# First projections of two mixer layers as three products of high and low parts, with some low parts made by GpSimd

## What is computed

```
h   = norm-modulated rows: x * (1 + scale) + shift, from "ada" rows     768 x 1024
all = h @ w_in[l]                                                      1024 x 3840
      columns: q, f, b  three 256-wide inputs of a gated scan (a)
               ai       256, the scan's values
               b, c, d  three 512-wide sets of heads (queries, keys, values); cv 256, c's values
               g0, g1   1024, the output gate
y_a = decayed scan in both directions over q, f, b, ai
y_b, y_c, y_d = three kinds of attention, over tokens and context
x   = layer_norm(alpha * x + gate * ((concat(y_a..y_d) * silu(g)) @ w_out[l]))
```

## Time and profile before

| | us |
|---|---|
| three runs, median | 2365.77 |
| lowest, highest | 2362.79, 2371.43 |
| profiled execution, its own time | 2367.96 |
| its span, first to last instruction | 2365.9 |
| TensorE busy (matmuls) | 2090.8 (88%) |
| VectorE, ScalarE, GpSimd busy | 1153.6, 727.3, 56.7 |
| mean granted clock of TensorE | 0.94 of 2.4 GHz |

### The profile page before, as it was taken

The page is one execution under the profiler, slowest core; times in us unless marked ns, Lnnn a source line. Parts: engine busy times, 40 slices in busy tenths (PEclk is TensorE's granted clock), DMA queues, the critical chain, the costliest instruction groups (busy, mean ns, idle before and its releaser), DMA issues.

```text
span 2365.9 us, 24945 instructions
## 1 busy us (share of the span) xinstructions
PE 2090.8 (88%) x9184; PEld 1341.3 (57%) x9184; DVE 1153.6 (49%) x2688; ACT 727.3 (31%) x1612; POOL 56.7 (2%) x98
## 2 busy tenths in 40 slices
PE   5888998999789698898997859968899997999999
PEld 2644655544344364565554424535478885887887
DVE  1284273545445548164655365773644444333333
ACT  2212224544330122234543111113542323223222
POOL 2000000000000000000000200000000000000000
PEclk9899999999789899999998979987899998999999
DMA  8111011000451211111000512112033331333331
GB/s 259 35 34 48 23 36 36 10 27 27 152 214 54 50 54 36 36 45 36 26 11 10 161 47 63 48 42 54 1 89 98 91 106 54 90 97 98 98 97 64
DMA packets 149144, 157.18 MB, mean 66 GB/s; under 512 B 5725, under 2 KB 110337, under 8 KB 149025
## 3 DMA queue, kind: packets, MB, share of 16 engines
q1 hardware_dynamic: 142592, 135.81, 18.8%
q0 software_dynamic: 6432, 19.78, 3.0%
HBM read 151.37 MB, written 4.19 MB: 66 GB/s over the span
## 4 chain that ended last, share of the span: by engine, by line
PE 73%; DVE 16%; ACT 5%; issue 3%; DMA 2%; POOL 1%; DVEq 0%; ACTq 0%; SPq 0%; POOLq 0%
PE psum L704 15%; PE psum L1115 9%; PE psum L1116 9%; PE psum L1117 9%; PE psum L879 5%; PE psum L716 5%; PE psum L731 4%; PE psum L1013 4%; PE psum L917 3%; PE psum L893 3%; PE psum L667 2%; DVE stats L1860 2%; ACT arena L1380 1%; PE psum L749 1%; ACT arena L1212 1%
## 5 line engine op out<-in xcount | busy, mean ns | idle before, releaser
L704 PE MATMUL psum<-arena 128*128 128x512 f32 (+2 forms) x1536 | 557.4, 521 | 8.6 <-ACT arena L1212 4.6
L1212 ACT ACTIVATE arena<-psum 128x256 f32<-128x256 f32 (+6 forms) x524 | 205.8, 421 | 789.5 <-PE psum L667 236.7
L704 PEld LDWEIGHTS psum<-arena 128*128 128x128 f32 x1536 | 294.9, 200 | 234.2 <-issue 205.8
L1115 PE MATMUL psum<-part,part 128*128 128x512 f32 x896 | 351.6, 392 | 10.8 <-DVE part L2191 8.8
L1116 PE MATMUL psum<-part,part 128*128 128x512 f32 x896 | 351.2, 392 | 0.0
L1117 PE MATMUL psum<-part,part 128*128 128x512 f32 x896 | 350.9, 392 | 0.0
L2187 DVE TENSOR_TENSOR part<-arena,part 128x1024 fp32r<-128x1024 f32 x112 | 137.3, 1226 | 251.5 <-ACT part L1212 251.5
L1860 DVE TENSOR_REDUCE stats<-psum 128x1 f32<-128x768 f32 (+6 forms) x208 | 138.8, 709 | 164.6 <-PE psum L879 163.2
L1212 ACT ACTIVATE part<-arena 128x1024 fp32r<-128x1024 f32 (+1 forms) x176 | 151.4, 895 | 202.1 <-PE psum L1117 140.9
L1115 PEld LDWEIGHTS psum<-part,part 128*128 128x128 f32 x896 | 169.6, 189 | 47.4 <-issue 12.2
L1117 PEld LDWEIGHTS psum<-part,part 128*128 128x128 f32 x896 | 169.5, 189 | 35.4
(11 more groups left out here) (253 smaller groups left out, 1929.9 us busy)
## 6 DMA issues: line engine op xcount, KB each, us to landing
arena<-in_w_in SPq DMA_DIRECT2D x72, 512.0 KB, 4.3
arena<-in_w_mlp SPq DMA_DIRECT2D x64, 512.0 KB, 3.9
arena<-in_w_ada SPq DMA_DIRECT2D x48, 512.0 KB, 6.1
arena<-in_w_gate SPq DMA_DIRECT2D x32, 512.0 KB, 4.1
arena<-in_w_out SPq DMA_DIRECT2D x24, 512.0 KB, 3.7
arena<-in_w_in SPq DMA_DIRECT2D x20, 256.0 KB, 3.1
arena<-in_w_branch SPq DMA_DIRECT2D x8, 512.0 KB, 4.2
arena<-in_x POOLq DMA_DIRECT2D x4, 512.0 KB, 9.1
```

The source lines that it names most:

```text
L704: mm = pe.matmul(bank(b)[:, c0:c1], lhs[:, k, m * P:(m + 1) * P], ring.view(tag, l, k // 2)[:, k % 2, c0:c1], start=k == 0, stop=k == kt - 1)
L1115: pe.matmul(dst, lo, x_hi_, start=first, stop=False)
L1212: return act.activation(dst, src, ACT.Copy)
```

## The change

The q, f, b, ai, b, c, cv and d products of both layers (not the gate products, not `w_out`) become three products of fp32r parts each.

- **h**: modulation writes rows into `gated`; ScalarE copies them to `h_hi` (in h_t's place) and VectorE subtracts in place, giving `h_lo` (`split_rows`). At the attention stage VectorE adds the two again (`whole_rows`) for the gate products, tile by tile.
- **weights**: per layer 22 blocks (13 and 9; ai and cv now in 2 blocks of 4 k instead of 4 of 2). ScalarE makes every high part, in space that is free at the time (`HI_PLACES`). The low part goes into the ring slot: 6 + 5 by VectorE (the next stage's first block, and `SPLIT_WITH` more beside the hg products), 7 + 4 by GpSimd (`SPLIT_BEFORE`: before which tile of the stream).
- **order**: two tiles of the stream come ahead of the scan, then 18 fillers on 14 steps (t = 0) and 11 on 9 (t = 1) in place of 20 and 13 on 14. In t = 1 ScalarE may write key rows only after the last d product.
- the arena becomes three tensors at the same addresses.

```diff
-    def rows(key, w, c0, n):
+    def rows(key, w, c0, n, per=2):
         v = w.rearrange("(k p) n -> p k n", p=P)
-        for i in range(KT // 2):
-            ring.add(key + (i,), v[:, 2 * i:2 * i + 2, c0:c0 + n], (2, n))
+        for i in range(KT // per):
+            ring.add(key + (i,), v[:, per * i:per * i + per, c0:c0 + n], (per, n))
...
+                rows(("ai", l), w, C_AI, 256, 4)
...
+        HI_PLACES = (("free", "o", "v0", "v1", "q0", "q1", "free", "o", "v0", "v1", "q0", "q1", "v0"),
+                     ("free", "q0", "q1", "s0", "s1", "s2", "free", "s0", "s1"))
+        SPLIT_BEFORE = ({1: (6,), 2: (7,), 3: (8,), 6: (9, 10), 12: (11, 12)}, {1: (5,), 2: (6,), 6: (7, 8)})
+        SPLIT_WITH = (5, 4)
+        def block_before(l, t, j):
+            place = HI_PLACES[t][j]
+            earlier = [input_blocks(l, t)[i] for i in range(j) if HI_PLACES[t][i] == place]
+            if t == 1 and j == 0:
+                earlier = [input_blocks(l, 0)[i] for i in range(13) if HI_PLACES[0][i] == place]
+            return earlier[-1] if earlier else None
+        def parts_made(key):
+            t = 1 if key[0] in ("cv", "d") or key[0] == "hg" and key[2] == 1 else 0
+            beside = any(input_blocks(key[1], t).index(key) in js for js in SPLIT_BEFORE[t].values())
+            return (lo_pool if beside else lo_dve).at(key)
+        def input_parts(key):
+            n = ring.number(*key)
+            t = 1 if key[0] in ("cv", "d") or key[0] == "hg" and key[2] == 1 else 0
+            hi = hi_slots[HI_PLACES[t][input_blocks(key[1], t).index(key)]]
+            return [ap.rearrange("p (k n) -> p k n", k=ring.dims[n][0]) for ap in (hi, ring_lo[n % N_SLOTS])]
...
+            def product_of_parts(tag, l, m, b, last, c0, c1, first):
+                per = SLOT // WIDTH[tag]
+                for k in range(KT):
+                    key = (tag, l, k // per)
+                    hi, lo = input_parts(key)
+                    if first and k % per == 0:
+                        pe.wait_ge(*parts_made(key))
+                    x_hi_, w_hi, w_lo = h_hi[:, k, m * P:(m + 1) * P], hi[:, k % per, c0:c1], lo[:, k % per, c0:c1]
+                    pe.matmul(bank(b)[:, c0:c1], h_lo[:, m, k, :], w_hi, start=k == 0, stop=False)
+                    pe.matmul(bank(b)[:, c0:c1], x_hi_, w_lo, start=False, stop=False)
+                    mm = pe.matmul(bank(b)[:, c0:c1], x_hi_, w_hi, start=False, stop=k == KT - 1)
+                    if last and k % per == per - 1:
+                        mm.then_inc(mm_done(("weights", ring.number(*key))), 1)
...
-                        pe.wait_ge(*ring.landed("hg", l, t, name))
+                        pe.wait_ge(*lo_dve.at(("hg", l, t, name)))
                     last = (name, s) not in [(x[0], x[1] - 1) for x in hg_tiles(l)]
                     open_bank(s)
+                    hi, lo = input_parts(("hg", l, t, name))
                     for k in range(KT):
-                        mm = pe.matmul(bank(s)[:, 0:t1 - t0], ring.view("hg", l, t, name)[:, k, :], h_t[:, k, t0:t1], start=k == 0, stop=k == KT - 1)
+                        mm = product_3(bank(s)[:, 0:t1 - t0], hi[:, k, :], lo[:, k, :], h_hi[:, k, t0:t1], h_lo[:, t0 // P:t1 // P, k, :], k == 0, k == KT - 1)
...
+                        if tag == "g0":
+                            pe.wait_ge(*whole_dve.at("h", l, m))
...
+            def split_rows(l, m):
                 if l > 0:
                     act.wait_ge(*product_ready("out1", l - 1, m, last_q_of(l - 1) - 1))
-                v, b = 0 if m < LT else 1, 4 + (2 * m) % 4
-                for j in range(4):
-                    x = act.activation(h_t[:, j, m * P:(m + 1) * P], bank(b)[:, j * P:(j + 1) * P], ACT.Identity,
-                                       bias=ada_t[:, l, j, v:v + 1], scale=ada_t[:, l, 8 + j, v:v + 1])
-                x.then_inc(h_act(("h", l, m)), 1)
+                act.wait_ge(*h_act.at("h", l, m))
+                act.wait_ge(*h_dve.at("h", l, m))
+                copy(h_hi[:, :, m * P:(m + 1) * P], h_rows[:, m]).then_inc(xhi_act(("h", l, m)), 1)
+            def split_input(l, t, j):
+                key = input_blocks(l, t)[j]
+                act.wait_ge(*ring.landed(*key))
+                if block_before(l, t, j) is not None:
+                    act.wait_ge(*mm_done.at("weights", ring.number(*block_before(l, t, j))))
+                copy(input_parts(key)[0], ring.view(*key)).then_inc(hi_act((key,)), 1)
...
+                    if n < SPLIT_WITH[t]:
+                        split_input(l, t, n + 1)
...
+                        if t == 1:
+                            act.wait_ge(*mm_done.at("weights", ring.number("d", l, KT // 2 - 1)))
...
+                    for j in SPLIT_BEFORE[t].get(p, ()):
+                        split_input(l, t, j)
...
-                    alongside(scan(l, t), 14, beside, 20 if t == 0 else 13)
+                    next(beside)
+                    alongside(scan(l, t), 14 if t == 0 else 9, beside, 18 if t == 0 else 11)
+                    if t == 0:
+                        split_input(l, 1, 0)
...
+            def split_rows(l, m):
+                dve.wait_ge(*xhi_act.at("h", l, m))
+                dve.tensor_tensor(h_lo[:, m], h_rows[:, m], h_hi[:, :, m * P:(m + 1) * P].bitcast(F32), ALU.subtract).then_inc(xlo_dve(("h", l, m)), 1)
+            def whole_rows(l, m):
+                cols = slice(m * P, (m + 1) * P)
+                dve.tensor_tensor(h_t[:, :, cols], h_hi[:, :, cols].bitcast(F32), h_lo[:, m].bitcast(F32), ALU.add).then_inc(whole_dve(("h", l, m)), 1)
+            def split_input(l, t, j):
+                key = input_blocks(l, t)[j]
+                hi, lo = input_parts(key)
+                dve.wait_ge(*hi_act.at(key))
+                dve.tensor_tensor(lo, ring.view(*key), hi.bitcast(F32), ALU.subtract).then_inc(lo_dve((key,)), 1)
...
-                for _ in range(8 * last_q_of(l)):
+                whole_rows(l, 0)
+                for i in range(8 * last_q_of(l)):
+                    if i % 4 == 0 and i // 4 + 1 < last_q_of(l):
+                        whole_rows(l, i // 4 + 1)
...
+                            if l < DEPTH - 1 and m >= 2:
+                                split_rows(l + 1, m - 2)
...
+                    split_rows(l + 1, last_q - 2)
                     modulate(l + 1, last_q - 1)
+                    split_rows(l + 1, last_q - 1)
+                    split_input(l + 1, 0, 0)
...
             for m in range(TT):
+                if m >= 1:
+                    split_rows(0, m - 1)
                 modulate(0, m)
+            split_rows(0, TT - 1)
+            split_input(0, 0, 0)
...
-                    for tag, m in stream_tiles(t):
+                    for p, (tag, m) in enumerate(stream_tiles(t)):
+                        for j in SPLIT_BEFORE[t].get(p, ()):
+                            key = input_blocks(l, t)[j]
+                            hi, lo = input_parts(key)
+                            pool.wait_ge(*hi_act.at(key))
+                            pool.tensor_tensor(lo, ring.view(*key), hi.bitcast(F32), ALU.subtract).then_inc(lo_pool((key,)), 1)
                         if tag in HEADS and LT <= m < last_q_of(l):
                             nq = HEADS[tag][0] * HEADS[tag][2]
                             q_dst = {"b": q_b, "c": q_c, "d": q_d}[tag][:, m, :]
```

More of the change, by code:

```diff
@@ L238, in build, with __init__ @@
         class Region:
-            def __init__(self, start, size):
-                self.start, self.size, self.at = start, size, 0
+            def __init__(self, start, size, tensor, first):
+                self.start, self.size, self.at, self.tensor, self.first = start, size, 0, tensor, first
             def reset(self):
@@ L247, in cut @@
                 assert self.at + n <= self.size, (self.at, n, self.size)
-                ap = base[:, self.start + self.at:self.start + self.at + n]
+                ap = self.tensor[:, self.first + self.at:self.first + self.at + n]
                 self.at += n
@@ L315, in build @@
         att = R_WORK.cut(2, TT, P)
-        key_rows, states = R_WORK.cut(TT + LT + 2 * CT, P), R_WORK.cut(TT + 4, P)
+        states = R_WORK.cut(TT + 4, P)
+        key_rows_at = R_WORK.start + R_WORK.at
+        key_rows = R_WORK.cut(TT + LT + 2 * CT, P)
         e_q, e_k = R_WORK.cut(2, SEQ), R_WORK.cut(2, CTX)
-        R_WORK.cut(2 * TT * SEQ + 2 * CT * CTX - (4 * TT + LT + 2 * CT + 4) * P - 2 * TOK)
-        q_s, kf_s, kb_s, o_a = R_WORK.cut(TOK), R_WORK.cut(TOK), R_WORK.cut(TOK), R_WORK.cut(TT, 256)
+        free_at = R_WORK.start + R_WORK.at
+        R_WORK.cut(SLOT)
+        q_s, kf_s, kb_s = R_WORK.cut(TOK), R_WORK.cut(TOK), R_WORK.cut(TOK)
+        o_a_at = R_WORK.start + R_WORK.at
+        o_a = R_WORK.cut(TT, 256)
+        h_hi = part(R_HT.start, KT * TOK).rearrange("p (k t) -> p k t", k=KT)
+        h_lo = part(R_G.start, KT * TOK).rearrange("p (m k n) -> p m k n", m=TT, k=KT)
+        h_rows = gated.rearrange("p m (k n) -> p m k n", k=KT)
```

(13 more changed lines are left out.)

52 lines of the change are left out of this document (35 added, 17 removed).

## The result

The changed kernel takes 2389.26 us (median of 4, 2385.6 to 2392.19), the kernel before 2368.6 beside it (4 runs, the three shown ahead and one more): ratio 1.0092, 95% interval 1.0076 to 1.0107. The forecast was 2351 with a range of 2320 to 2382. The profiled execution has a span of 2386.4 us against 2365.9 before.

What follows compares the result with a forecast made beforehand. TensorE carries 73% of the chain, but VectorE sets the b stretch, so little of 83 us saved TensorE time arrives. Stage, scan, attention and layer-end terms sum to -15.2 us: 2365.8 to 2351, range 2320 to 2382.

Steps and rivals of the forecast that it cites:

- Products of 256 columns: fp32r tile products at 256 columns: one each 0.120 us, 2.88 us a tile, 0.57 less than f32.
- rival 2: 256-column products: the weight load doesn't hide, 0.189 us a product; +53 us, 2404 in all; chance 0.08.
- Stage 1's ring: Modulation, stage 1: high copy, VectorE's split and modulate wait on each other, 3.7 us a tile; +15.2 us.
- hg at t = 0: hg products of each layer's first scan: shorter from f on, less 1.05 us for f's high copy; -3.0 us each.
- whole_rows: Attention: two sums (2.46 us) behind the first maxima delay TensorE's gate product and next scores; +3.1 us a layer.
- the end of layer 0: Layer 0's last stretch: splits ahead of the last z, then chained splits, modulates and high copies; +10.4 us.
- P: Duration of one GpSimd subtraction that makes a low part; taken as 2.5 us.
- TensorE's wait in the first c tile: Layer 0, t = 0: TensorE stands 6 us for GpSimd's blocks, then pays some 3 at half clock; +9 us.
- hg at t = 1: hg products of the second scans, where nothing holds them: -6.0 us in layer 0, -5.4 in layer 1.
- The second scans: Behind hg, t = 1: VectorE sets the pace and no tiles cover the tail; -7.0 us (layer 0), -2.6 (layer 1).
- The first scans: Behind hg, t = 0: b begins earlier (-5.5 us in layer 0), c tiles shorter; -7.0 (layer 0), -13.0 (layer 1).
- rival 1: Scans: GpSimd's subtractions hold VectorE for their whole duration; +14 us in all, 2365; chance 0.22.

Runs made afterwards that it cites:

- e3: Changed kernel with all sums that make h whole moved to the end of the second scan, ahead of the barrier: 2382.4 us, ratio 1.0047.
- e1: Changed kernel without GpSimd's low parts; those 22 blocks use the high part a second time: 2367.1 us, ratio 0.9991.
- e5: Kernel before, plain f32 products, with only the new order of tiles and levels: 2384.3 us, ratio 1.0062.
- e9: Changed kernel, second scans only: one tile in front instead of two, the others over eleven steps instead of nine: 2374.1 us, ratio 1.0029.
- e11: Changed kernel with GpSimd instead of VectorE making h's low parts in stage 1: 2384.0 us, ratio 1.0064.
- e6: Changed kernel with the old order of tiles and levels in each layer's first scan: 2394.2 us, ratio 1.0103.
- e10: Changed kernel with early whole sums, wider stage 1 ring, c's low parts by VectorE, early d2 and d3, later second-scan tiles: 2356.8 us, ratio 0.9938.

## Why the prediction was wrong

**Right, with their numbers.** Products of 256 columns 0.120 us apart: the q product of stage 2 starts them at 71.75, 71.86, 71.98, 72.10.

```profile
71.75 0.28 PE L1189 MATMUL psum<-part,part 128*128 128x256 f32 x1
71.86 0.28 PE L1190 MATMUL psum<-part,part 128*128 128x256 f32 x1
71.98 0.28 PE L1191 MATMUL psum<-part,part 128*128 128x256 f32 x1
```

So rival 2 is out. Stage 1's ring (+15.7 for +15.2; ScalarE's high copies start at 45.12 and 48.80, 3.68 apart, each behind an idle 1.23), hg at t = 0 (-4.1 and -3.4 for -3.0 each), `whole_rows` (+3.6 and +2.6 for +3.1; e3 gives it back), the end of layer 0 (+9.7 for +10.4). P is 2.40 us (median of 22) for 2.5. TensorE's wait in the first c tile came, ended by GpSimd, and not in layer 1:

```profile
201.30 0.80 PE L773 MATMUL psum<-part,part 128*128 128x512 f32 x1 [4.29 <-POOL part L2466]
```

It is 4.29 us for the 6 I gave it. hg at t = 1 gave 4.3 of 6.0 in layer 0: the first products ran at the lower clock, behind 2.73 us of idle for the split at the barrier.

**The step that failed: the scans behind hg, priced from busy time.** I took VectorE's work as if it would run without waits once begun, and let TensorE's saving arrive where waits stood before. By stretches, with the low parts for nothing (e1) against my sum without its GpSimd charges: 7.0, 10.0, 9.1 and 0.2 us too little arrived, 26 of the 33; the other 7 are GpSimd's.

The second scans: "The d tiles are spent by the sixth level ... + 2 for a low clock in a tail without tiles". e(0) comes at hg + 21.0 in layer 0 (forecast 20.7, before 16.4), and the work on it was not 51.6 us but 68.0 (306.9 to 374.9): 4.3 of GpSimd's hold, and waits of 3.1, 3.2, 1.1, 1.6, 2.3 and 2.1 us, one at almost each level, since level, exponentials, decays and level products are a chain over three engines. Then the tail, 14.6 us for 13.4. e5 has the order by itself: +7.9 and +6.3. e9 takes the front tile and the early spending back and gets 7.4 and 5.2 us. In layer 1 that cost is there too, but e1 is within 0.2 us of my -2.6: my number there has no sum behind it ("that part is at 91 us already"), and that it fits is luck.

The first scans: "VectorE begins on b 34.9 us after hg, now 40.4 ... -5.5". It begins 40.3 behind hg, as before. That step was nearly right by itself: in e1 it is 35.9 (layer 1: 34.3, before 39.1), and the hold in level 1 took the 4.4 us back. I had set against rival 1 that VectorE has gaps of 3 us at c0, c1. The gap is there (3.27 us, to 127.78), but the blocks come too late for it: the first of the two subtractions starts at 129.13, with VectorE at work again.

**Waits that I let vanish.** In c I booked six tiles at 1.43 and 4 us of vanished waits. Behind the stall, from the level of 206.5 to the scan's last step at 239.0, the kernel after takes 32.5 us, before 35.9: four tiles give 5.7, and new waits of 1.5 and 0.6 take 2 back, while the wait of 3.09 us for VectorE in front of that step is the same to the hundredth before and after. Here a shorter tile mostly moves TensorE to the next wait. The largest miss of the first scans lies in this part: from VectorE's first c tile to the end, e1 is 5.6 us (layer 0) and 1.9 us (layer 1) shorter than before, and I had booked 10.3 and 7.9.

**Rival 1 was right in its mechanism.** Removing the GpSimd work gives 24 us (e1), with 17 in my sum (10, 5 and 2 by the stretches; the charge of 2 us that I named for t = 1 has no term of its own there): its own excess is some 7 us, not the 36. The Trainium skill (SBUF — State Buffer, SBUF: two separate sides) says that the common port pair is locked for the whole instruction, and that VectorE's side needs it when both inputs come from SBUF. The trace agrees on both: 2.32 us for a 128x2 instruction of 0.17, and modulations from PSUM untouched (e11). I gave this rival 0.22 and charged 1 or 2 us a scan where whole holds, 4.3 us, were due: the 0.2 us of the earlier trace rows were the rest of a short copy, and I took them for the price.

**As a sum.** Behind hg, kernel before: 490.9. The order alone +15.8 (e5: 506.8). The products, with low parts for nothing, -35.8 (e1: 471.0) out of 60 of TensorE's time. GpSimd's low parts +24.0 (495.0). This takes e5's cost as the same under both kinds of product. e9's 12.6 for the second scans bears that out (e5: 14.2); in the first scans e6 differs (with short products the order gains 0.3 and 3.0, in e5 it gains 0.8 and costs 2.1). By e9 and e6 the order costs some 9 us and the products give 29, so the split between these two is known to some 6 us only.

**What stays open.** In layer 1's first scan even e1 is only 5.9 us shorter; TensorE's own saving there is 17. The windows show 12.3 us less busy time and 6.5 more idle, and 6 of the missing 9 us lie behind VectorE's first c tile, but no run takes single waits of that stretch away. And e10's first scans keep 2 to 3 us of gain where e1 has 10 and 6.

## What to carry to other kernels

A faster engine is worth what the chain around it lets through: price each stretch by its waits from end to end, test a new interleaving by itself on the old kernel, and spread the filler so that the last serial steps still have some beside them. GpSimd is no free engine beside VectorE: give it SBUF work while VectorE idles or reads PSUM, and count its whole duration, not VectorE's small instruction, wherever VectorE works on SBUF. A ring through two engines is cut by letting one of them run a tile ahead (6 us for two moved lines), and work that has to be done before the next stage belongs in front of the barrier, where engines idle.
